# Expert tokens gathered into transposed form for eight experts at once, and small loads issued by another queue

## What is computed

```python
sh1, sc1, gt1, sh2, sc2, gt2 = ada_modulation(c, w_ada, b_ada)
h = rms_norm(x, g_mix) * (1.0 + sc1) + sh1          # then the mixer, z = h @ w_in
...
idx, w = route(t, w_router, b_router)                # 8 of 64 experts a token
def block(acc, xs):
    tok, w, e = xs
    xb = t[tok]                                      # gather of an expert's tokens
    yb = (silu(xb @ w_gate[e]) * (xb @ w_up[e])) @ w_down[e]
    return acc.at[tok].add(yb * w[:, None])
```

## Time and profile before

| what | value |
|---|---|
| median of 3 runs | 929.48 us (927.88 to 931.46) |
| the profiled execution | 932.22 us, its span 930.4 us |
| PE busy | 860.4 us, 92% of the span |
| first gate/up matmul of the expert stage | at 327.49 us |
| last down matmul | about 882.5 us |
| from one body to the next | 14.86 us |

### The profile page before, as it was taken

How to read it: one execution, slowest core, us unless ns; L and a number is a source line. 1 busy time by engine, 2 the same in 40 slices (tenths; PEclk the granted TensorE clock), 3 DMA queues, 4 the chain that set the end, 5 groups by cost and what they waited for, 6 DMA issues and landing times.

```text
span 930.4 us, 13928 instructions
## 1 busy us (share of the span) xinstructions
PE 860.4 (92%) x4436; PEld 470.1 (51%) x4437; DVE 268.6 (29%) x797; ACT 247.9 (27%) x484; POOL 88.4 (10%) x189
## 2 busy tenths in 40 slices
PE   7699999797898999999999999999999999999962
PEld 3199983534686744444444444444444444444521
DVE  2354426435226611111211121121212112121118
ACT  2353424134113312131222212121222213121231
POOL 3000011200022000101101010101101010100000
PEclk9889989798798999999999999999999999999977
DMA  8934447452526369099995999699996999999183
GB/s 326 362 133 160 182 181 276 151 181 92 222 81 263 103 272 376 40 366 415 428 425 245 406 427 426 271 371 420 427 425 254 397 427 426 426 427 426 77 302 157
DMA packets 55370, 273.84 MB, mean 294 GB/s; under 512 B 12720, under 2 KB 13056, under 8 KB 27312
## 3 DMA queue, kind: packets, MB, share of 16 engines
q1 hardware_dynamic: 42064, 258.23, 68.3%
q0 software_dynamic: 6560, 12.55, 3.6%
q10 hardware_dynamic: 6720, 2.70, 1.1%
HBM read 261.34 MB, written 22.07 MB: 305 GB/s over the span
## 4 chain that ended last, share of the span: by engine, by line
PE 85%; DVE 5%; DMA 4%; ACTq 2%; issue 2%; ACT 1%; SPq 0%; POOL 0%; POOLq 0%; DVEq 0%
PE psum L1174 27%; PE psum L1193 13%; PE psum L1150 10%; PE psum L870 8%; PE psum L1157 4%; PE psum L1071 4%; DMA expert_w<-in_w_exp_down 3%; PE psum L840 3%; PE psum L1099 2%; PE psum L1166 2%; PE psum L1089 1%; ACTq L480 1%; PE psum L1183 1%; PE psum L1226 1%; PE psum L825 1%
## 5 line engine op out<-in xcount | busy, mean ns | idle before, releaser
L1174 PE MATMUL psum<-expert_w,xg 128*64 128x512 f32 x1184 | 263.9, 598 | 3.4 <-DMA expert_w<-in_w_exp_down 1.7
L1174 PEld LDWEIGHTS psum<-expert_w,xg 128*64 128x64 f32 x1184 | 85.8, 137 | 150.1 <-issue 149.4
L1193 PE MATMUL psum<-expert_w,hidT 128*64 128x512 f32 x592 | 135.2, 599 | 0.0
L1150 PE MATMUL psum<-h2hl,sel 128*128 128x512 f32 x380 | 97.8, 403 | 0.5 <-ACT acc L616 0.5
L1150 PEld LDWEIGHTS psum<-h2hl,sel 128*128 128x128 f32 x380 | 68.4, 188 | 43.7 <-issue 30.0
L634 ACT ACTIVATE silg<-psum 128x256 f32<-128x256 f32 x37 | 14.2, 384 | 260.9 <-PE psum L1174 260.9
L1193 PEld LDWEIGHTS psum<-expert_w,hidT 128*64 128x64 f32 x592 | 39.3, 137 | 69.6 <-issue 69.6
L1597 DVE SCALAR_TENSOR_TENSOR hid<-psum,ws,silg 128x256 f32<-128x256 f32 x37 | 17.9, 483 | 195.7 <-ACT silg L634 195.7
L623 ACT COPY xs<-psum 128x512 f32<-128x512 f32 x76 | 44.5, 586 | 58.1 <-PE psum L1150 58.1
L1607 DVE COPY y_slot<-psum 128x512 f32<-128x512 f32 x37 | 25.6, 691 | 117.7 <-PE psum L1193 117.7
L1157 PE MATMUL psum<-ident,xs 128*128 128x128 f32 x304 | 47.7, 280 | 0.5 <-ACT xs L623 0.2
(11 more groups left out here) (370 smaller groups left out, 846.5 us busy)
## 6 DMA issues: line engine op xcount, KB each, us to landing
expert_w<-in_w_exp_gate SPq DMA_DIRECT2D x64, 1024.0 KB, 9.9
expert_w<-in_w_exp_up SPq DMA_DIRECT2D x64, 1024.0 KB, 11.9
expert_w<-in_w_exp_down SPq DMA_DIRECT2D x64, 1024.0 KB, 12.7
ring<-in_w_ada SPq DMA_DIRECT2D x24, 1024.0 KB, 7.0
pair<-in_w_in SPq DMA_DIRECT2D x6, 2048.0 KB, 9.6
y_rank<-y_d SPq DMA_DIRECT2D x8, 1024.0 KB, 12.9
pair<-in_w_out SPq DMA_DIRECT2D x2, 2048.0 KB, 8.2
x_tok<-in_x_prompt SPq DMA_DIRECT2D x2, 512.0 KB, 4.1
```

The lines of the kernel that those rows point to most:

```text
L1150: last = mm(bank[q][:, :], sel[:, t // 2, :, :], h2hl[:, t, 4 * q:4 * q + 4, :], start=t == 0, stop=t == 4)
L1174: last = mm(bank[3][CAP * x:CAP * x + CAP, :].rearrange("p (g n) -> p g n", g=2), xg[:, k, CAP * x:CAP * x + CAP], expert_w[2 * u + x][:, ...
L1193: last = mm(bank[4 + half][CAP * x:CAP * x + CAP, :], hidT[:, i, CAP * x:CAP * x + CAP], expert_w[2 * u + x][:, 2, o:o + 512], start=i == ...
```

## The change

- **Gather.** For the first 64 slots of the eight experts of a *quad* (four pairs), PE now loads the tokens' columns `h2hl[:, t, k, :]` as weights and moves `sel4` (8 x 64 = 512 columns): the result is the width chunk k of the gathered tokens, already transposed. `token_chunk(k)` is five matmuls; eight chunks serve a quad. The chunks of the next quad are made two a body, in the last body of each pair. ACT copies each chunk into `xgT`. Only further bodies still gather and transpose in the old way.
- **Selections.** DVE makes `sel4` for a whole quad at once (`select_quad`: eight selections after the last body of a quad's fourth pair, two quads ahead); `wp` is copied in each body.
- **Slots.** `ws` and `row_f` now have a column a pair and are read out at once (`slot_values`); the three `slots` matmuls follow gate/up.
- **Loop.** The loops over pairs are unrolled by eight pairs, not two.
- **Before the loop.** All eight chunks, twelve `slots` matmuls, and eight `wp` copies of quad 0 are made before the first body.
- **Front.** Nine small DMAs, `pastf` and `states` are issued by POOL, not ACT, after POOL has cleared `ada_row`. DVE copies two of the four first modulation rows. The first `w_in` piece comes as two DMAs, and the first half-group waits for its own half alone.
- **Tail.** `gt2B` is loaded by SP after the last body, not by POOL before the loop.

```diff
+QUAD = 4
+SLOTS4 = QUAD * 2 * CAP
+DUMMY = 4 * QUAD
...
+            if n == FIRST_WIN:
+                for q in range(2):
+                    sp.dma_start(dst[:, :, 256 * q:256 * q + 256], src[:, :, 256 * q:256 * q + 256]).then_inc(ring_in[slots_of[n][q]], 16)
...
+        sp.wait_ge(s["y_act"], num(sp, n))
+        for g in range(2):
+            sp.dma_start(gt2B[:, g, :], gt2_d[g].partition_broadcast(P)).then_inc(s["gt2_in"], 16)
...
-            for dst, src in small[3:]:
-                act.dma_start(dst, src).then_inc(s["small_in"], 16)
-        act.dma_start(pastf[:, :, :], cache_fox_logf[0, 0].rearrange("(j p) h -> p j h", p=P)).then_inc(s["cache_in"], 16)
...
-            for j in range(4):
+            for j in range(4 if r else 2):
                 act.copy(ada_row[32 * j:32 * j + 2, :], bank[b][32 * j:32 * j + 2, :]).then_inc(s["ada_row"], 1)
...
+        def token_chunk(n, g, p, q):
+
+            act.wait_ge(s["xs_ps"], num(act, n * 2 + (KC + q + 1)))
+            k = 2 * p + q
+            last = act.copy(xgT[g][k // 4][:, k % 4, :], bank[q][:, :])
...
+        act.wait_ge(s["fin_ok"], KC)
+        with act.Fori(0, PAIRS // (2 * QUAD)) as it:
+            for m in range(2 * QUAD):
...
+        def token_chunk(k):
+
+            for t in range(5):
+                last = mm(bank[k % 2][:, :], h2hl[:, t, k, :], sel4[:, t // 2, :, :, :], start=t == 0, stop=t == 4)
+            last.then_inc(s["xs_ps"], 1)
...
+            pe.wait_ge(s["sel_ok"], num(pe, n + 2))
+            pe.wait_ge(s["ws_ok"], num(pe, n + 1))
+            if last_of_pair:
+                if p == 0:
+                    pe.wait_ge(s["sel4_ok"], num(pe, quad + 2))
+                slots(sel4[:, :, p, :, :], p).then_inc(s["slots_ps"], 1)
+                token_chunk(2 * p)
+            else:
+                slots(sel, p).then_inc(s["slots_ps"], 1)
+                gather(0)
+                gather(1)
             pe.wait_ge(s["hid_ok"], num(pe, n + 1))
             for i in range(2):
                 last = tr(bank[6][:, P * i:P * i + P], hid[:, i::2], ident[:, :])
             last.then_inc(s["hidT_ps"], 1)
-            gather_T(n + 1, 0)
-            gather_T(n + 1, 1)
+            if last_of_pair:
+                token_chunk(2 * p + 1)
+            else:
+                gather_T(e, 0)
+                gather_T(e, 1)
...
+        pe.wait_ge(s["sel4_ok"], 1)
+        for k in range(KC):
+            if k >= 2:
+                pe.wait_ge(s["xs_ok"], k - 1)
+            token_chunk(k)
+            if k == 3:
+                pe.wait_ge(s["sel_ok"], 1)
+                for p in range(QUAD):
+                    last = slots(sel4[:, :, p, :, :], p)
...
+        def select_quad(b, gathered):
+
+            for p in range(QUAD):
+                chosen = experts_of(b + p)
+                if p == 0 and gathered is not None:
+                    dve.wait_ge(s["xs_ps"], gathered)
+                for x, e in enumerate(chosen):
+                    last = dve.tensor_tensor(sel4[:, :, p, x, :], iota[:, 0:CAP].unsqueeze(1).broadcast_to([P, 3, CAP]),
+                                             posm[:, :, bass.ds(e, 1)].broadcast_to([P, 3, CAP]), ALU.is_equal)
+            last.then_inc(s["sel4_ok"], 1)
...
             dve.tensor_copy(y_slot[:, 0:512], bank[4][:, :]).then_inc(s["y_dve"], 1)
+            if last_of_pair and p == QUAD - 1:
+                select_quad(b + (QUAD + 1), num(dve, n * 2 + (KC + 2)))
```

More of the change, by code:

```diff
@@ L272, in layer @@
         loads[sl[0]] += 1
+        if n == KC:
+            loads[sl[1]] += 1
         turn.append(loads[sl[0]])
@@ L285, in piece @@
         return ring[slots_of[n][0]] if pieces[n][1] == 1 else pair[slots_of[n][0] // 2]
+    second_turn = 1 + sum(1 for n in range(FIRST_WIN) if slots_of[n][0] == slots_of[FIRST_WIN][1])
     SHARED = FRONT
@@ L641, in act_block @@
             act.copy(y_slot[:, 512:D], bank[5][:, :]).then_inc(s["y_act"], 1)
-        slots_in(0)
-        gathered(0)
-        with act.Fori(0, PAIRS // 2) as it:
-            for u in range(2):
-                each_block(act, it * 2 + u, lambda n, j, last: act_block(n))
+        for k in range(KC):
+            act.wait_ge(s["xs_ps"], k + 1)
+            act.copy(xgT[0][k // 4][:, k % 4, :], bank[k % 2][:, :]).then_inc(s["xg_ok" if k == KC - 1 else "xs_ok"], 1)
+        act.wait_ge(s["fin_ok"], KC)
+        with act.Fori(0, PAIRS // (2 * QUAD)) as it:
+            for m in range(2 * QUAD):
+                g, p, b = m // QUAD, m % QUAD, it * (2 * QUAD) + m
+                each_block(act, b, lambda n, e, j, last: act_block(n, e, g, p, last))
         for i in range(3):
@@ L689, in _ @@
         pool.wait_ge(s["consts"], 1)
+        pool.memset(ada_row[:, :], 0.0).then_inc(s["row_zeros"], 1)
+        pool.wait_ge(s["row_zeros"], 1)
+        with nc.allow_non_contiguous_dma(reason="vectors of a few hundred elements"):
+            for dst, src in small[3:]:
+                pool.dma_start(dst, src).then_inc(s["small_in"], 16)
+            pool.dma_start(pastf[:, :, :], cache_fox_logf[0, 0].rearrange("(j p) h -> p j h", p=P)).then_inc(s["state_in"], 16)
+        for c in range(2):
+            pool.dma_start(states[:, 4, c, :], state_gla[0, 0, 2 * c:2 * c + 2].rearrange("h k v -> (h k) v")).then_inc(s["state_in"], 16)
         pool.memset(qA[FD:FD + 2, :, :], 1.0).then_inc(s["ones_ok"], 1)
@@ L794, in _ @@
         pool.wait_ge(s["gt2_out"], 32)
-        pool.wait_ge(s["gu_ps"], 4)
-        pool.wait_ge(s["h2t_ps"], 6)
-        for g in range(2):
-            pool.dma_start(gt2B[:, g, :], gt2_d[g].partition_broadcast(P)).then_inc(s["tail_in"], 16)
         pool.memset(zero[:, :], 0.0).then_inc(s["y_gone"], 1)
@@ L1144, in _, with gather @@
         pe.wait_ge(s["table_ok"], 1)
-        def gather(n, q):
-            pe.wait_ge(s["sel_ok"], num(pe, n + 1))
+        def gather(q):
             for t in range(5):
@@ new lines, in slot_values, with dve_block @@
+        def slot_values(c, p):
+            for x in range(2):
+                half = slice(CAP * x, CAP * x + CAP)
+                dve.tensor_reduce(ws[half, c:c + 1], bank[2][half, 8 * p + x:8 * p + 4:2], AX, ALU.add)
+                last = dve.tensor_reduce(row_f[half, c:c + 1], bank[2][half, 8 * p + 4 + x:8 * p + 8:2], AX, ALU.add)
+            return last
+        def dve_block(n, b, g, p, j, last_of_pair):
+            c = QUAD * g + p
+            chosen = experts_of(b + QUAD if last_of_pair else b)
+            at = None if last_of_pair else dve.snap((j + 1) * CAP)
+            dve.wait_ge(s["xs_ps"], num(dve, n * 2 + KC))
+            if not last_of_pair:
+                select_further(chosen, at)
+            weights_of(chosen, p).then_inc(s["sel_ok"], 1)
@@ L1613, in _ @@
+        last.then_inc(s["sel_ok"], 1)
         for k in range(KC):
```

173 lines of the change are left out of this document (97 added, 76 removed).

## The result

The changed kernel is slower: 952.76 us median (951.98 to 955.01) against 930.47 us, a ratio of 1.0232 with a 95% interval of 1.0209 to 1.0254. The forecast was 926 us, a gain, and its range ended at 938. The profiled execution took 952.78 us with a span of 951.0.

A forecast was written before the change was run, and what follows sets the result against it. PE and the weight DMAs were taken as two bounds within 2% of each other. Terms -6.9 - 1.8 + 9.0 - 4.7 + 0.5 = -3.9 us took the profiled 932.22 to 928.3, hence a median of 926; range 913 to 938.

The forecast's parts named there:

- instruction fetch: Rival, chance 0.14: the longer loop over pairs is fetched again each turn, stalling PE at each pair; 953 or +65 us.
- My 953 us for that case: Instruction fetch costing 1.8 us a pair in the loop: PE's cycle of six pairs becomes 107.6 us, +27 us.
- the sign to look for: Sign against the forecast: PE idle as its own issue, at each pair or loop turn, with many more fetch packets.
- Transposes: Last bodies in the expert stage: each of 32 loses 1.20 us, 38.4 us of PE's time; body 13.66 us.
- The weights, -6.9 and -1.8 before them: Expert loop: load cycles of six pairs shrink to 102.5 us, -6.9 in all; bodies before the first release, -1.8.
- Loop entry, +9.0: Before the first body: selections, table loads and extra matmuls delay the first gate/up by 9.0 us (+7 to +11).
- Each quad: After each fourth pair: late selections make PE wait 1.5 us, seven times; costed at nothing, 10 us if uncovered.
- Front, -4.7: Before the expert stage: modulation rows copied earlier on two engines, so hhi starts at 38.2, not 42.90: -4.7 us.
- Tail, +0.5: After the last body: SP's two gt2B broadcasts before the first read-back of scattered rows, +0.5 us (0 to +2.5).

The follow-up runs named there:

- light weights: Changed kernel with its loops over pairs written out, each down weight in the loop loading only its first quarter: 905.06 us, ratio 0.9744.
- chunks for four experts in a loop that fits: Changed kernel with QUAD = 2 (256-column chunks, four a body) and loops unrolled by four pairs: 923.76 us, ratio 0.9921.
- the direct comparison: Kernel with four-expert chunks, loops by four pairs, gt2B loaded by POOL before the loop, against the same with SP's late load: 921.11 us against 923.76.
- by eight pairs: Kernel before the change with only its loops over pairs unrolled by eight pairs instead of two: 953.83 us, ratio 1.023.

## Why the prediction was wrong

The step that failed is the rival *instruction fetch*, in its chance and in its shape; the sum had no term for it, that is, it put the turns of the longer loop at nothing. Of the 24.5 us between the forecast for the profiled execution (928.3) and its 952.78, the part up to the last gate/up holds 24.0: forecast -7.5, measured +16.5. I had the numbers, 2,350 instructions where 620 had run without a second fetch, and gave it 0.14 because "no row shows such a stall or its price". The absence of a row was no evidence: a loop of 620 instructions can't show one. And I priced it as a stall at each pair, with a part hidden under the loads. It comes at each turn of the loop, three times, all at once (gaps of 5, 10 and 9 us, and a slower clock behind), so that 0.9 us of slack a pair hides almost nothing of it. My 953 us for that case met the result by luck. What the prediction did get right is the sign to look for: idle PE marked as its own issue at each turn of the loop, with many more fetch packets. Since it had itself worked out that the long loop no longer fits, a stall at three turns should have had most of the chance. The price I could only have guessed, but 1.3 us a turn were enough to use up the forecast gain of 3.9.

The other steps, in order:

- *Transposes:* right. The body is 13.5 us (forecast 13.66), and with light weights the gain comes through.
- *The weights, -6.9 and -1.8 before them:* right in total where nothing is fetched again, and partly by luck. The part of the sum up to the last gate/up was -7.5; with chunks for four experts in a loop that fits it is -8.3 (532.2 against 540.5). But its parts were mis-sized against each other: up to the last gate/up of pair 2 it gained 4.6 us where I had 1.8 (1.7 of them are the first gate/up, 7.09 us instead of 8.78), the three cycles 3.2 instead of 4.5 (103.2, 103.1 and 103.0 against my 102.5), the last stretch 0.5 instead of 1.2. In the changed kernel the stalls turned the whole into +16.5: 24.8 us more than in the fitting loop with four experts, 16.3 more than in its own written-out form, which pays the price of straight code.
- *Loop entry, +9.0:* right. 330.33 - 327.49 = 2.8, and without the front's gain of 5.6, +8.4. These are single profiles: the first gate/up began at 325.4 to 328.7 in five that have the old front and the old gathering, and at 323.6 in the one with the new front alone, against which the entry is only +6.7. With four experts it is +3.6 (first gate/up at 325.51).
- *Each quad:* right. The late selections are there, and the loads cover them as assumed; uncovered the seven of them cost 10.6 us, against my 10.
- *Front, -4.7:* right, slightly more: `hhi` at 37.34 instead of 42.90, -5.6, and it passes through to the end.
- *Tail, +0.5:* mis-sized. It is +2.0 in the changed kernel and 2.8 in the direct comparison, above my end of 2.5: the broadcasts delay the issue of the read-back by 2.5 us (7.1 against 4.6 behind the last down projection), and do not only fill a gap.

With the fitting loop's -8.3 in place of the turns', the changed kernel's own parts give 2.8 - 8.3 - 0.75 + 2.0 = -4.2 us against my -3.9. The sum that I worked out was nearly right, with errors in the loop's terms and the tail that offset each other, and what stood outside the sum decided.

## What to carry to other kernels

Before unrolling a loop further, count the instructions of one turn on each engine and compare them with the longest loop that the profile shows to run without new fetch packets: here 1,260 on PE ran free and 2,350 cost 16 to 25 us in three turns, about two to three times the 8.3 us that the new gathering gives the loop. Make the unit of the optimisation small enough for that (four experts instead of eight), rather than the loop long enough for the unit; writing the loop out is no way around, since it cost some 4 us in each of two kernels. Where loads lie 2% under the engine you relieve, expect those 2% at most, and look for what stands idle at the ends instead: the front's small changes together gave 5.6 us, as much as the new gathering in its best form net of its longer entry (8.3 + 0.7 - 3.6).

## What the runs showed of the hardware

- Two engines' fetch stalls run side by side: removing PE's (957.1 us) or DVE's (952.7) gave nothing against both (952.8), removing both gave 12.
- A fetch at a turn took far longer than its transfer. PE's packets on q8 followed each other at 6 us (630, 636 and 642 us; 771, 777 and 783), each with some 0.9 us of one DMA engine, while the DMA engines were at a share of 1.01. PE's gaps, 4.3 to 9.9 us, span the wait for one or two of them; DVE's reached 11.7 us in the same place. That the packets wait behind the weights' traffic is likely but not shown: no run has both the long loop and light loads.
- Behind gaps of 4.79 us (by eight pairs) and 9.89 us (the changed kernel) gate/up took 9.70 and 9.73 us instead of 7.04 to 7.09, at a granted clock of 0.85 and 0.83 over the body (1.00 in the undisturbed one). So a stall is paid for a second time, by 2.7 us. Shorter waits can cost it too: in the kernel with four experts a gate/up behind 2.15 us of waiting for weights took 8.79 us at one place and 7.09 at another.
- Straight code has a price on a kernel whose DMA queues are full: 1.0049 (1.003 to 1.0069) for the kernel before, and 0.9921 to 0.9955 for the one with four experts. The Trainium skill, "Runtime: NRT & Kernel Launch", Instruction fetch mechanics, holds full unrolling to be preferable where possible; here the loop that fits was faster in both pairs measured.
